# Moving the on-chip buffers of a three-block kernel to multiples of 1024 bytes

## The chip, the core and the metric

The kernel runs on one core of a Trainium2 chip. Its time is the device time in microseconds (us) of one execution, from start to end. TensorE is called PE below, its weight loads PEld, VectorE DVE, ScalarE ACT, GpSimd POOL and SyncE SP. SBUF is the on-chip memory that the compute engines work from, PSUM the memory that matmuls write.

## What is computed

Three transformer-like blocks run one after the other on 256 tokens of width 2048, in fp32, with one layer each: a block with latent attention and a bidirectional recurrence, one with a convolution, pooling, a Fourier mix and a gated MLP, and one with two attentions and a gated MLP. The time goes for the most part into dense products with large weights, such as these two of the second block (the reference, cut):

```python
def first_block(x, g_pre, w_in, ...):
    h = rms_norm(x, g_pre)
    proj = h @ w_in
    ...
def second_block(x, ..., w_gate, w_up, w_down, ...):
    ...
        hid = jax.nn.silu(jnp.einsum("bsd,df->bsf", x, w_gate[i])) * \
            jnp.einsum("bsd,df->bsf", x, w_up[i])
        ffn = jnp.einsum("bsf,fd->bsd", hid, w_down[i])
        ...
def third_block(x, c, positions, w_ada, b_ada, ...):
        mod = jax.nn.silu(c) @ w_ada[l] + b_ada[l]
        ...
        x = x + g2 * conv_ffn(h2, w_up[l], conv_w[l], conv_b[l], w_down[l])
    return rmsnorm(x, final_norm_g)
```

## The kernel before

Activations stand with features on the 128 partitions and the 256 tokens along the row, so a chunk of 128 features is 128 x 256 fp32 values, 1024 bytes in each partition. Nearly all activations live in one large SBUF array, `work`; functions `w(at, ...)` and `own(name, at, ...)` cut named pieces out of it, `at` in fp32 words from its start. `own` gives a piece a tensor of its own at the same address, mostly of type fp32r, the reduced fp32 format in which PE takes one pass over the columns.

Weights come in slots of 8192 bytes per partition (1 MB in all) through a ring of four slots, `ring`. SP issues the transfer of slot n when PE has used slot n - 4. Where the product is split (lines 442 to 444, function `by_parts`), ACT rounds each half slot to fp32r into `ring_hi` (line 1054), DVE subtracts that from the weights and leaves the rest in place of them, in `ring_parts`, which is the ring under a second type (line 1569). The activations are split in the same way into a `_hi` and a `_lo` tensor. Each tile of 128 x 128 weights then takes three fp32r matmuls of 256 columns, in the order L442 (high weights by high activations), L443 (high weights by low activations), L444 (low weights by high activations), each with a load of its own weights before it, four column tiles m for each of 16 or 44 chunks. The other dense products (`by_feature`, line 414, and the gates in line 603) are plain fp32 out of the ring. Weights are the stationary operand and activations the moving one.

The 24 us to 300 us of the run are the first block's input products in split form (moving `h1_hi`, `h1_lo`, weights `ring_hi1` and `ring_parts`); 480 to 1100 us the recurrence in a loop over eight pairs of heads, small fp32 matmuls (lines 629 to 721) between ACT and DVE; 1110 to 1500 us plain fp32 products and the convolution; from 1540 us to the end split products again, with `mix_hi`, `x_hi`, `hid_hi`, `hs_hi` and `h_hi` as moving operands and `ring_hi` as weights. In three stretches POOL fetches 96 tiles `work<-in_ada` of 1 MB, on which DVE works in line 1584.

All orders are written out by hand: each engine's program is a fixed sequence with semaphores, and addresses take no part in it. The allocator `sb(...)` hands out SBUF from the bottom up, each buffer at a multiple of 32 bytes; the order of the calls in the code sets the addresses.

Of the kernel before, what the change touches and what calls it, by code (L numbers as in the profile page):

```python
# [17 lines left out]
P = 128  # L18
T = 256
D = 2048  # L20
DC = D // P
COLS = 512
KPS = 4
SLOT = KPS * COLS
# [23 lines left out]
TRI = 384  # L48
# [70 lines left out]
NPAR = [sum(w for _, w in b) for b in PARAMS]  # L119
# [21 lines left out]
N_CONST = max(N_1, N_3 + 4 * T)  # L141
# [57 lines left out]
def build_program(nc, a):  # L199
# [3 lines left out]
    def sb(name, shape, dt=F32):  # L203
        return ctx.enter_context(nc.sbuf_tensor(name, shape, dt))
# [6 lines left out]
        return sems[name]  # L211


    ring_at = -(-nc.sbuf_base // 32) * 32
    ring = sb("ring", [P, RING, SLOT])
    ring_parts = nc.alloc_sbuf_tensor_at("ring_parts", [P, RING, SLOT], F32R, offset=ring_at)
    CON = sb("con", [P, N_CONST])
    PR = sb("par", [P, max(NPAR)])
    X = sb("resid", [P, DC, T])
    MOD = sb("mod", [P, 96])  # L220
    RED = sb("red", [P, 2, T])
    STD = sb("std", [P, 2, T])
    work_at = -(-nc.sbuf_base // 32) * 32
    W = sb("work", [P, WORK])
    PS = ctx.enter_context(nc.psum_tensor("ps", [P, 8, 512], F32))

    def w(at, *shape):

        n = int(np.prod(shape))
        v = W[:, at:at + n]  # L230
        names = "abcde"[:len(shape)]
        if len(shape) == 1:
            return v
        return v.rearrange(f"p ({' '.join(names)}) -> p {' '.join(names)}", **{k: s for k, s in zip(names[1:], shape[1:])})

    def own(name, at, *shape, dt=F32R):


        return nc.alloc_sbuf_tensor_at(name, [P, *shape], dt, offset=work_at + 4 * at)[:]

    def con(name, n, at=0):
        off = {**OFF_ALL, **OFF_1, **OFF_3}[name]
        return CON[:, off + at:off + at + n]

    def par(name, k=0, n=1):
        return PR[:, PAR[name] + k:PAR[name] + k + n]

# [29 lines left out]
    H1_LO = [own("h1_lo0", 12288, 8, T), own("h1_lo1", 29184, 8, T)]  # L277
    NKK = X[:, 0:8, :]
    TW = X[:, 8:12, :]
    SG1 = X[:, 12:16, :]  # L280
    LW = X[:, 14:16, :].rearrange("p a (b n) -> p (a b) n", b=2)

# [39 lines left out]
    GU, GU2, GU3 = w(30720, 4, T), w(31744, 4, T), own("gu", 32768, 4, T, dt=F32)  # L322
    P2, P2_HI, P2_LO = w(33792, 2, T), own("p_hi", 34304, 2, T), own("p_lo", 33792, 2, T)
    BROW = w(20736, 2 * COLS)
    HI = own("ring_hi", 35504, 4, SLOT // 2)


    Q_SB, K_SB, V_SB = w(4096, 8, T), w(6144, 8, T), w(8192, 2, WIDTH)
# [2 lines left out]
    SBB = w(15424, 4, 4, TRI)  # L331
    ROT = CON[:, N_3:N_3 + 4 * T].rearrange("p (c t) -> p c t", t=T)
    TURN, TURNI, ANG = w(30720, 4, T), w(30720, 4, T).bitcast(I32), w(31744, 4, T)
    TURN_IX, TURN_DS = w(8192, 4, T), w(17472, 4, T)
    REL = w(25664, 4, TRI)
    LG, PTR = [w(25664, 4, TRI), w(21568, 4, TRI)], [w(27200, 4, TRI), w(23104, 4, TRI)]
    SCORE, LEFT, SBIAS = w(29760, TRI), w(30144, TRI), w(30528, TRI)
    TOP, SM3 = w(30912, 8), w(30920, 64)
    O3, O3_LO = w(31008, DC, T), own("o3_lo", 31008, DC, T)
    SQ3 = w(15424, DC, T)  # L340
    NORM3 = w(4096, DC, T)
    HS_HI = own("hs_hi", 21568, DC, T)
    HID3_HI, HID3_LO = own("hid3_hi", 4096, FF3_CHUNKS, T), own("hid3_lo", 15360, FF3_CHUNKS, T)
    H3_HI, H3_LO = own("h3_hi", 26624, DC, T), own("h3_lo", 0, DC, T)
    UP3 = w(30720, 8, T + 2)
# [19 lines left out]
    def _(sp):  # L365
        for k in range(4):
            sp.dma_start(X[:, 4 * k:4 * k + 4, :], a["x"][:, 4 * k:4 * k + 4, :]).then_inc(S(f"x_loaded{k}"), 16)
        for k in range(RING):
# [17 lines left out]
    def _(pe):  # L386
# [90 lines left out]
        def sum_over_features(bank, k):  # L477

            t.wait(S("red_ready"), 1)
            t.give(mm(PS[:, bank, 0:T], ones, RED[:, k, :], start=True, stop=True), S("sum_ready"))  # L480

# [10 lines left out]
        def sum_reduced(bank, k):  # L492


            t.wait(S("red_ready"), 1)
            mm(PS[:, bank, 0:T], ones, RED[:, k, :], start=True, stop=False)

# [258 lines left out]
        sum_chunks(4, SQ, 12, 4, False, True)  # L756
        xc = lambda k: X[:, k, :]

# [267 lines left out]
    def _(act):  # L1026
# [34 lines left out]

        act.dma_start(CON[:, 0:N_ALL], a["const1"][:, 0:N_ALL]).then_inc(S("first_loaded"), 16)
        act.dma_start(PR[:, 0:NPAR[0]], a["params1"]).then_inc(S("first_loaded"), 16)
        for k in range(4):
            act.wait_ge(S(f"x_loaded{k}"), 16)
            t.give(A(SQ[:, 4 * k:4 * k + 4, :], X[:, 4 * k:4 * k + 4, :], ACT.Square), S("squared"))
        act.dma_start(CON[:, N_ALL:N_1], a["const1"][:, N_ALL:N_1]).then_inc(S("const_loaded"), 32)
        act.wait_ge(S("first_loaded"), 32)
# [179 lines left out]
        act.wait_ge(S("x_ready"), DC)  # L1248
        act.dma_start(PR[:, 0:NPAR[1]], a["params2"]).then_inc(S("params_loaded"), 16)
        act.dma_start(CON[:, N_ALL:N_3], a["const3"]).then_inc(S("params_loaded"), 16)  # L1250
        act.dma_start(P2, a["p"]).then_inc(S("params_loaded"), 16)
# [84 lines left out]
        act.wait_ge(S("x1_ready"), 2 * DC)  # L1336
        act.dma_start(PR[:, 0:NPAR[2]], a["params3"]).then_inc(S("params_loaded"), 16)

        def modulated(n, shift, hi):

            for k in range(DC):
                act.wait_ge(S("scaled"), (2 + n) * DC + k + 1)
                A(hi[:, k, :], NORM3[:, k, :], ACT.Identity, bias=MOD[:, shift + k:shift + k + 1])
                A(H[:, k, :], NORM3[:, k, :], ACT.Identity, bias=MOD[:, shift + k:shift + k + 1]).then_inc(S("h3_ready"), 1)
                if n == 0 and k in (7, 11):
# [148 lines left out]
    def _(gp):  # L1494
# [22 lines left out]
        with gp.Fori(0, PAIRS) as i:  # L1517
            gp.wait_ge(S("stage_free"), i + 1)
            gp.nop()
            for dst, src in ((RC, RR_), (KC, KK_), (NC_, NKK)):  # L1520
                gp.tensor_copy(dst, src[:, bass.ds(i, 1), :].rearrange("p a t -> p (a t)"))
            gp.tensor_copy(PP, PR[:, bass.ds(PAR["pair"] + i * 8, 8)])
            gp.tensor_copy(VD, VV_[:, bass.ds(i, 1), :].rearrange("p a (c s) -> p (a c) s", s=CH).unsqueeze(2)
# [14 lines left out]
    def _(v):  # L1538
# [8 lines left out]
        def add_chunks(src, n, k):  # L1547

            t.give(v.tensor_reduce(RED[:, k, :], src.rearrange("p c t -> p t c"), AX.X, ALU.add), S("red_ready"))

# [26 lines left out]
        def modulation(first, count):  # L1577


            for n in range(first, first + count):  # L1580
                run, slot, loads = ADA_AT[n]
                x = ADA[run][0][slot]
                v.wait_ge(S(f"ada_loaded{slot}"), 16 * loads)
                v.tensor_tensor_reduce(x, x, ADA[run][1], 1.0, 0.0, ALU.mult, ALU.add, MOD[:, n:n + 1])\  # L1584
                    .then_inc(S("ada_used"), 1)
# [313 lines left out]
        for j in range(2):  # L1899
# [10 lines left out]
            with v.Fori(0, TAPS - 1) as i:  # L1910
                for m in range(4):
                    c = 4 * j + m
                    v.wait_ge(S("conv_step"), i * 4 + (4 * TAPS * j + m + 1))
                    stt(ACC[:, c, :], W[:, bass.ds(i + (c * (T + TAPS - 1) + 1), T)],
                        PR[:, bass.ds(i * 8 + (PAR["taps"] + 8 + c), 1)],
                        ACC[:, c, :], ALU.mult, ALU.add).then_inc(S("conv_step"), 1)
# [31 lines left out]
        v.wait_ge(S("ada_used"), ADA_COLUMNS)  # L1948
        t.give(tt(MOD[:, :], MOD[:, :], par("b_ada", 0, 96), ALU.add), S("mod_ready"))
        def angles(part):  # L1950
# [105 lines left out]
        for gain, at_ in (("n1_g", 16), ("n2_g", 64)):  # L2056
            ins = stt(MOD[:, at_:at_ + DC], MOD[:, at_:at_ + DC], 1.0, par(gain, 0, DC), ALU.add, ALU.mult)
        step(ins)

        def scaled_norm(n, at_, hi):  # L2060

            invert(0)
            for k in range(DC + 2):
                if k < DC:
                    t.give(stt(NORM3[:, k, :], X[:, k, :], MOD[:, at_ + k:at_ + k + 1], STD[:, 0, :], ALU.mult, ALU.mult),
                           S("scaled"))
# [487 lines left out]
```

## Time and profile before

| | |
|---|---|
| median of 3 runs | 3747.72 us (3746.31 to 3749.8) |
| profiled execution, its own time | 3751.21 us |
| its span, first to last instruction | 3749.9 us |
| mean granted TensorE clock | 0.983 |
| PE busy / PEld busy | 3567.7 / 3365.8 us |
| DVE busy / ACT busy | 2232.4 / 1410.3 us |
| DMA, mean | 174 GB/s |

The profile is of one execution. The matmuls of PE are pipelined and their ends are modelled: 280 ns is how long one is in the array, not how often one starts. How often one starts is read from the starts in the timeline, or from the number of matmuls in a window in which PE never waits.

### The profile page before, as it was taken

To read this page: it belongs to the slowest core of one execution; us is meant where nothing else is said; L and a number is where in the kernel's file an instruction comes from. 1 tells how busy PE (TensorE), PEld (TensorE's weight loads), DVE (VectorE), ACT (ScalarE), POOL (GpSimd) and SP (SyncE) were. 2 spreads that over 40 slices of the span, in tenths; PEclk is the share of its full clock that TensorE was granted. 3 is DMA by queue.
4 is the path that set the end of the run, shared out by engine and by line. 5 is a ranking of instruction groups with operands and counts; after the bars stand their busy time and mean duration, and the time that the engine had idled before them with its cause. 6 is when DMAs were issued, how large, how long until landed. Compare 5 with 4: busy or idle time off the path is not lost.

```text
span 3749.9 us, 63400 instructions
## 1 busy us (share of the span) xinstructions
PE 3567.7 (95%) x26060; PEld 3365.8 (90%) x26060; DVE 2232.4 (60%) x3034; ACT 1410.3 (38%) x1688; POOL 76.1 (2%) x155
## 2 busy tenths in 40 slices
PE   8997889999999999889999999998998999999998
PEld 8996788888888886689999999997987899999998
DVE  7865455555447569765555554455566667777545
ACT  5441123332220000454444433345355454444443
POOL 0000000000000100000000000000000000000000
PEclk9999999999999999989999999999999999999999
DMA  8647611111137984435555555553442455555554
GB/s 309 258 172 301 233 52 67 57 48 48 59 122 275 385 330 164 146 134 180 186 183 190 181 192 193 193 185 113 160 154 96 156 185 183 190 180 189 191 188 151
DMA packets 91728, 654.13 MB, mean 174 GB/s; under 512 B 10177, under 2 KB 10817, under 8 KB 13122
## 3 DMA queue, kind: packets, MB, share of 16 engines
q1 hardware_dynamic: 74736, 540.05, 40.2%
q0 software_dynamic: 14256, 103.82, 7.0%
q10 hardware_dynamic: 2594, 8.15, 0.6%
q8 instruction: 116, 1.90, 0.2%
q14 instruction: 26, 0.21, 0.0%
HBM read 649.88 MB, written 2.10 MB: 174 GB/s over the span
## 4 chain that ended last, share of the span: by engine, by line
PE 88%; DVE 6%; ACT 3%; issue 1%; DMA 1%; ACTq 0%; DVEq 0%
PE ps L442 19%; PE ps L444 19%; PE ps L443 19%; PE ps L414 11%; PE ps L603 6%; PE ps L677 2%; PE ps L665 2%; PE ps L473 1%; PE ps L488 1%; DVE ring_parts L1569 1%; DMA work<-in_ada 1%; PE ps L721 1%; PE ps L712 1%; ACT work L1216 1%; DVE work L1584 0%
## 5 line engine op out<-in xcount | busy, mean ns | idle before, releaser
L1569 DVE TENSOR_TENSOR ring_parts<-ring,ring_hi 128x1024 fp32r<-128x1024 f32 x810 | 977.0, 1223 | 792.4 <-ACT ring_hi L1054 781.8
L1054 ACT ACTIVATE ring_hi<-ring 128x1024 fp32r<-128x1024 f32 x810 | 852.3, 1061 | 1102.8 <-PE ps L444 1090.9
L443 PE MATMUL ps<-h_lo,ring_hi 128*128 128x256 f32 x2624 | 735.4, 280 | 0.0
L442 PE MATMUL ps<-h_hi,ring_hi 128*128 128x256 f32 x2112 | 598.7, 283 | 26.7 <-DVE ring_parts L1569 22.3
L444 PE MATMUL ps<-h_hi,ring_parts 128*128 128x256 f32 x2112 | 595.0, 282 | 0.0
L443 PEld LDWEIGHTS ps<-h_lo,ring_hi 128*128 128x128 f32 x2624 | 496.6, 189 | 1.4 <-issue 1.2
L442 PE MATMUL ps<-x_hi,ring_hi 128*128 128x256 f32 x1664 | 467.2, 281 | 5.8 <-DVE x_lo L1591 4.5
L444 PE MATMUL ps<-x_hi,ring_parts 128*128 128x256 f32 x1664 | 467.3, 281 | 0.0
L443 PE MATMUL ps<-x_lo,ring_hi 128*128 128x256 f32 x1664 | 463.6, 279 | 0.0
L442 PEld LDWEIGHTS ps<-h_hi,ring_hi 128*128 128x128 f32 x2112 | 400.4, 190 | 29.9 <-DVE ring_parts L1569 24.5
L444 PEld LDWEIGHTS ps<-h_hi,ring_parts 128*128 128x128 f32 x2112 | 401.2, 190 | 0.0
L444 PE MATMUL ps<-hid_hi,ring_parts 128*128 128x256 f32 x1392 | 390.1, 280 | 0.0
L442 PE MATMUL ps<-hid_hi,ring_hi 128*128 128x256 f32 x1392 | 389.8, 280 | 0.0
L443 PE MATMUL ps<-hid_lo,ring_hi 128*128 128x256 f32 x1392 | 387.0, 278 | 0.0
L442 PEld LDWEIGHTS ps<-x_hi,ring_hi 128*128 128x128 f32 x1664 | 312.9, 188 | 6.4 <-issue 4.8
L414 PE MATMUL ps<-work,ring 128*128 128x256 f32 x1440 | 313.7, 380 | 2.6 <-DVE work L1873 2.6
L443 PEld LDWEIGHTS ps<-x_lo,ring_hi 128*128 128x128 f32 x1664 | 313.1, 188 | 0.0
L444 PEld LDWEIGHTS ps<-x_hi,ring_parts 128*128 128x128 f32 x1664 | 312.2, 188 | 0.0
L414 PEld LDWEIGHTS ps<-work,ring 128*128 128x128 f32 x1440 | 274.4, 191 | 42.1 <-DVE work L1873 3.0
L1584 DVE CUSTOM_DVE_ANT_0 work<-work 128x2048 f32<-128x2048 f32 x96 | 218.6, 2289 | 85.3 <-DMA work<-in_ada 85.2
L443 PEld LDWEIGHTS ps<-hid_lo,ring_hi 128*128 128x128 f32 x1392 | 261.0, 188 | 0.0
L442 PEld LDWEIGHTS ps<-hid_hi,ring_hi 128*128 128x128 f32 x1392 | 260.8, 187 | 0.0
(422 smaller groups left out, 5420.2 us busy)
## 6 DMA issues: line engine op xcount, KB each, us to landing
ring<-in_weights SPq DMA_DIRECT2D x511, 1024.0 KB, 4.8
work<-in_ada POOLq DMA_DIRECT2D x96, 1024.0 KB, 9.0
work<-in_c_row POOLq DMA_DIRECT2D x3, 1024.0 KB, 4.9
resid<-in_lora ACTq DMA_DIRECT2D x9, 256.0 KB, 2.6
resid<-in_x SPq DMA_DIRECT2D x4, 512.0 KB, 6.8
resid<-in_x ACTq DMA_DIRECT2D x1, 2048.0 KB, 13.9
out<-work SPq DMA_DIRECT2D x4, 512.0 KB, 2.9
con<-in_const ACTq DMA_DIRECT2D x1, 1536.0 KB
```

Of the source, the lines that this page charges most:

```text
L414: ins = mm(PS[:, b + m // 2, (m % 2) * T:(m % 2 + 1) * T], ws[:, k, m * P:(m + 1) * P], rhs(kc), start=(kc == 0 and m % 2 == 0), stop=(kc ...
L442: mm(o, w_hi[:, k, cols], hi(kc), start=(kc == 0 and m % 2 == 0), stop=False, skip_group_check=True)
L443: mm(o, w_hi[:, k, cols], lo(kc), start=False, stop=False, skip_group_check=True)
L444: ins = mm(o, w_lo[:, 2 * half + k, cols], hi(kc), start=False, stop=(kc == last - 1), skip_group_check=True)
L473: ins = mm(PS[:, b + m, :], lhs(kc, m), ws[:, k, :], start=(kc == 0 and not biased), stop=(kc == per * KPS - 1), skip_group_check=True)
L488: ins = mm(PS[:, bank, 0:T], ones, src[:, k, :], start=(begin and k == first), stop=(end and k == first + count - 1))
L603: ins = mm(PS[:, m // 2, (m % 2) * T:(m % 2 + 1) * T], ws[:, k, m * P:(m + 1) * P], H[:, kc, :], start=(kc == 0 and m % 2 == 0), stop=(kc ...
L665: ins = mm(PS[:, 2 + 3 * d, c * P:(c + 1) * P], LS[:, d, c, :], XY[:, d, 0, c, :], start=True, stop=True)
L677: ins = mm(PS[:, 3 + 3 * d, c * P:(c + 1) * P], XY[:, d, 1, c, :], ZS[:, d, c, :], start=True, stop=True)
L1054: A(high_ring(n)[:, 2 * (e % 2) + half, :], ring[:, n % RING, half * (SLOT // 2):(half + 1) * (SLOT // 2)], ACT.Copy)\
L1569: tt(lo, x, high_ring(n)[:, e % 4, :].bitcast(F32), ALU.subtract).then_inc(S("lo_ready"), 1)
L1584: v.tensor_tensor_reduce(x, x, ADA[run][1], 1.0, 0.0, ALU.mult, ALU.add, MOD[:, n:n + 1])\
```

## The change

The calls that allocate SBUF stand in another order. The small buffers (`mod`, `par`, `con`) come first, then a pad of 544 bytes that nothing uses, then `red`, `std`, `resid`, the ring and the work area, and these five begin at multiples of 1024 bytes. Inside the work area four regions that did not begin at a multiple of 256 words from its start are moved to one: `HI` (the tensor `ring_hi`), the score buffers at 25664 and 21568, `O3`/`O3_LO`, and `HS_HI` with the second pair of score buffers. Each engine's instructions, their order, shapes and waits are the same in both programs; only addresses differ.

```diff
-    ring_at = -(-nc.sbuf_base // 32) * 32
+    MOD = sb("mod", [P, 96])
+    PR = sb("par", [P, max(NPAR)])
+    CON = sb("con", [P, N_CONST])
+    pad = -(-(-nc.sbuf_base // 32) * 32) % 1024 // 4
+    if pad:
+        sb("pad", [P, pad])
+    RED = sb("red", [P, 2, T])
+    STD = sb("std", [P, 2, T])
+    X = sb("resid", [P, DC, T])
+    ring_at = nc.sbuf_base
     ring = sb("ring", [P, RING, SLOT])
     ring_parts = nc.alloc_sbuf_tensor_at("ring_parts", [P, RING, SLOT], F32R, offset=ring_at)
-    CON = sb("con", [P, N_CONST])
-    PR = sb("par", [P, max(NPAR)])
-    X = sb("resid", [P, DC, T])
-    MOD = sb("mod", [P, 96])
-    RED = sb("red", [P, 2, T])
-    STD = sb("std", [P, 2, T])
-    work_at = -(-nc.sbuf_base // 32) * 32
+    work_at = nc.sbuf_base
     W = sb("work", [P, WORK])
+    assert ring_at % 1024 == 0 and work_at % 1024 == 0
...
-    HI = own("ring_hi", 35504, 4, SLOT // 2)
+    HI = own("ring_hi", 35328, 4, SLOT // 2)
...
-    REL = w(25664, 4, TRI)
-    LG, PTR = [w(25664, 4, TRI), w(21568, 4, TRI)], [w(27200, 4, TRI), w(23104, 4, TRI)]
+    REL = w(25856, 4, TRI)
+    LG, PTR = [w(25856, 4, TRI), w(21760, 4, TRI)], [w(27392, 4, TRI), w(23296, 4, TRI)]
...
-    O3, O3_LO = w(31008, DC, T), own("o3_lo", 31008, DC, T)
+    O3, O3_LO = w(31232, DC, T), own("o3_lo", 31232, DC, T)
...
-    HS_HI = own("hs_hi", 21568, DC, T)
+    HS_HI = own("hs_hi", 21760, DC, T)
```

Where the tensors stand, by the two built programs (bytes in a partition, and the remainder to 1024):

| tensor | before | remainder | after | remainder |
|---|---|---|---|---|
| ring, ring_parts | 1152 | 128 | 37888 | 0 |
| con | 33920 | 128 | 3488 | 416 |
| par | 47296 | 192 | 1536 | 512 |
| resid | 49248 | 96 | 21504 | 0 |
| red | 66016 | 480 | 17408 | 0 |
| work | 70112 | 480 | 70656 | 0 |
| ring_hi1 (first block) | 143840 | 480 | 144384 | 0 |
| h1_hi, h1_lo | 160224, 119264 | 480 | 160768, 119808 | 0 |
| x_hi, x_lo, mix_*, hid_*, h3_* | 160224 ... | 480 | 160768 ... | 0 |
| ring_hi (blocks two and three) | 212128 | 160 | 211968 | 0 |
| hs_hi | 156384 | 736 | 157696 | 0 |
| o3_lo | 194144 | 608 | 195584 | 0 |

A tile of 128 weight columns is 512 bytes, so column tiles with odd m stand 512 bytes further: `ring_hi` then has remainders 160 and 672 before, 0 and 512 after. In the recurrence the tiles XY, LS and ZS stand behind a buffer of 8 words, so they begin at multiples of 64 bytes before and 32 bytes past one after; the other tiles of `work` do the reverse.

## Rows read from the trace of the kernel before

**Rows 1.** The page's head: span, busy time of each engine, granted clock in 40 slices.

```profile
span 3749.9 us, 63400 instructions
PE 3567.7 (95%) x26060; PEld 3365.8 (90%) x26060; DVE 2232.4 (60%) x3034; ACT 1410.3 (38%) x1688; POOL 76.1 (2%) x155
PEclk9999999999999999989999999999999999999999
```

**Rows 2.** The page's chain of work that ended last, shares of the span.

```profile
PE 88%; DVE 6%; ACT 3%; issue 1%; DMA 1%; ACTq 0%; DVEq 0%
```

**Rows 3.** One line's instructions: L443, matmuls, by operand; min/median/max ns, first and last start.

```profile
L443 PE MATMUL ps<-h_lo,ring_hi x2624: 277/279/420, 24.5 to 3491.3; 128*128 128x256 f32 x188
...
L443 PE MATMUL ps<-x_lo,ring_hi x1664: 277/279/416, 1670.0 to 2456.3; 128*128 128x256 f32 x185
...
L443 PE MATMUL ps<-hid_lo,ring_hi x1392: 277/278/279, 2196.6 to 3734.4; 128*128 128x256 f32 x199
...
L443 PE MATMUL ps<-mix_lo,ring_hi x256: 277/279/416, 1552.1 to 1643.5; 128*128 128x256 f32 x128
...
L443 PE MATMUL ps<-o_lo,ring_hi x256: 276/281/283, 2886.7 to 2976.8; 128*128 128x256 f32 x128
...
L443 PE MATMUL ps<-p_lo,ring_hi x32: 277/278/279, 2193.8 to 2459.1; 128*128 128x256 f32 x32
```

**Rows 4.** Windows (start:end, length, busy and count by engine, clock, DMA share, GB/s).

```profile
core 0: us, PE busy (x) PEld busy (x) DVE busy (x) ACT busy (x) POOL busy (x), PEclk, DMA share, GB/s
60.00:100.00 40.00, 40.00 (x342) 40.00 (x341) 29.56 (x26) 15.97 (x17) 2.65 (x5) 1.00 0.89 334
2000.00:2400.00 400.00, 400.00 (x3398) 400.00 (x3398) 202.98 (x169) 167.76 (x158) 0.00 (x0) 1.00 0.54 190
2905.00:2975.00 70.00, 70.00 (x597) 70.00 (x596) 40.33 (x38) 28.53 (x28) 0.00 (x0) 1.00 0.54 190
```

**Rows 5.** The window 1250:1300, plain fp32 matmuls of L414, same columns.

```profile
1250.00:1300.00 50.00, 50.00 (x233) 44.03 (x232) 29.85 (x26) 3.88 (x4) 6.35 (x12) 1.00 1.01 421
```

**Rows 6.** Timeline of PE at 2900 us (start, us in the array, line, operands).

```profile
2899.91 0.29 PE L444 MATMUL ps<-hs_hi,ring_parts 128*128 128x256 f32 x1
2900.03 0.28 PE L442 MATMUL ps<-hs_hi,ring_hi 128*128 128x256 f32 x1
2900.16 0.28 PE L443 MATMUL ps<-o_lo,ring_hi 128*128 128x256 f32 x1
2900.27 0.28 PE L444 MATMUL ps<-hs_hi,ring_parts 128*128 128x256 f32 x1
2900.39 0.28 PE L442 MATMUL ps<-hs_hi,ring_hi 128*128 128x256 f32 x1
```

**Rows 7.** One line each: durations min/median/max of DVE and ACT work.

```profile
L1914 DVE SCALAR_TENSOR_TENSOR work<-work,par x240: 466/474/481, 1417.8 to 1515.6; 128x256 f32<-128x256 f32 x120
L1569 DVE TENSOR_TENSOR ring_parts<-ring,ring_hi x810: 1160/1225/1230, 22.8 to 3726.0; 128x1024 fp32r<-128x1024 f32 x162
L1054 ACT ACTIVATE ring_hi<-ring x810: 1039/1061/1072, 18.9 to 3724.9; 128x1024 fp32r<-128x1024 f32 x162
```

**Rows 8.** Groups by line and shape: busy us, mean ns, idle before.

```profile
L2270 DVE TENSOR_TENSOR uc<-uc 128x1024 f32<-128x1024 f32 x11 | 13.5, 1225 | 0.4
L1476 ACT ACTIVATE work<-uc 128x1024 f32<-128x1024 f32 x11 | 11.7, 1065 | 0.1
```

**Rows 9.** Matmuls of the recurrence, by line: min/median/max ns.

```profile
L665 PE MATMUL ps<-work x640: 275/275/348, 507.0 to 1077.2; 128*128 128x128 f32 x160
L670 PE MATMUL ps<-con,work x256: 272/273/273, 513.8 to 1078.1; 128*128 128x128 f32 x128
L629 PE MATMUL ps<-work x128: 272/275/275, 497.4 to 1050.7; 128*128 128x128 f32 x128
```

**Rows 10.** DMA in the window 320:400: GB/s in 40 slices of 2 us.

```profile
GB/s 57 418 49 0 66 274 258 406 422 365 385 406 414 426 426 426 426 422 422 426 422 418 410 418 266 299 414 365 385 176 422 8 0 33 299 193 0 127 410 418
```

**Rows 11.** Who waited for whom: us in total, times, longest us.

```profile
DVE work L1584 <- DMA work<-in_ada: 85.2, 52, 5.4
...
PEld ps L442 <- DVE ring_parts L1569: 29.3, 15, 7.4
```

## The prediction, made before the changed kernel was run

> **What bounds the kernel now.** The page's head first: PE is busy for 3567.7 of 3749.9 us at almost full clock, DVE for 60% and ACT for 38% [rows 1]. The chain of work that ended last agrees: 88% of it is PE, 6% DVE, 3% ACT, 1% DMA [rows 2]. So what counts is how often a matmul starts. The change leaves every instruction, its place and its waits as they are. It can move the time only through what an address does: to PE's two reads of SBUF (moving operand and next weights), to the reads and writes of DVE and ACT, or to where DMA lands.
>
> The rows then tell how many matmuls are exposed and how long one step takes. L443 stands for one of the three matmuls of each split tile; its six groups count 2624 + 1664 + 1392 + 256 + 256 + 32 = 6224 [rows 3], so there are 3 x 6224 = 18672 split matmuls of 256 columns. A step is the time from one start to the next, and the windows without a wait give it. In 2000 to 2400 us there are 3398 [rows 4]; each is in the array for about 0.28 us, so 0.28 / 0.118 = 2.4 of them began before the window. 400 / 3395.6 = 117.8 ns. The split matmuls thus take 18672 x 0.1178 = 2200 us, 59% of the span. The plain fp32 matmul of the same shape, which takes two passes over its columns, steps at 50 / (233 - 1.8) = 216.3 ns [rows 5], 108.1 ns a pass. A split matmul is one pass and takes 9.7 ns more than that. This surplus is the only thing in the profile that an address could be behind and that is large: 18672 x 9.7 ns = 181 us.
>
> **The change part by part.** *PE, split matmuls.* The trace already holds a natural experiment, since the operands stand differently in the three windows of [rows 4]. In 60:100 the moving tensors and `ring_hi1` have the same remainder to 1024 (480), so the offset between the two reads is 0 or 512 for two of three products. In 2000:2400 it is 480 against 160 or 672. In 2905:2975 the moving operands are at 736 and 608, the weights at 160 and 672. In all three, `ring_parts` is at 128 or 640. Their steps: 40 / (342 - 2.4) = 117.8, 117.8, and 70 / (597 - 2.4) = 117.7 ns. Three relations of moving to stationary address, one step. Inside a pattern of three the gaps do differ, 0.11, 0.12 and 0.13 us in [rows 6], but they make up for each other. Weights at a multiple of 64 bytes (`ring_parts`) and 32 bytes past one (`ring_hi`) both occur in each window, and the mean of the three lines is what is fixed. What the trace doesn't show is a moving operand of a 256-column split matmul at a multiple of 64, 256 or 1024: all stand 32 bytes past a multiple of 64. I bound this unseen case by the nearest rows: below by the pass of the plain matmul (108.1 ns, so -181 us), above by the gaps in [rows 6], 0.12 as the typical high one (+2.2 ns x 18672 = +41 us) and 0.13 as the extreme (+12.2 ns, +228 us). I take 0, since three of three relations gave the same step.
>
> *PE, plain matmuls.* In [rows 5] the moving operand is 32 bytes past a multiple of 64, the weights are 128 past a multiple of 1024, and a pass is already 108.1 ns, the shortest step here; nothing is left to gain. 0.
>
> *PE in the recurrence.* Here some tiles lose their place: XY, LS and ZS leave multiples of 64 while the rest of `work` reaches them. L665 reads only the former, L629 only the latter, both 275 ns for the same shape [rows 9]: 0 either way. The constants leave a multiple of 64 too. Transposes that move `con` show 273 ns against 275 [rows 9]; if they lose those 2 ns, with 256 of L670 and some 190 others of its kind (estimate), the loss is 450 x 2 ns = 0.9 us. I take +0.5.
>
> *DVE and ACT.* L1914, the convolution, reads its input at an offset that steps by 4 bytes through 30 places; all 240 take between 466 and 481 ns [rows 7]. So an offset of DVE is worth at most 15 ns in 474 and no multiple of 64 stands out. For the largest group: L1569, 1225 ns with the ring at a multiple of 64 and `ring_hi` off it [rows 7], against L2270, same shape, everything off it, 1225 ns [rows 8]. ACT: L1054 reads the ring, 1061 ns [rows 7]; L1476 reads `uc` off it, 1065 ns [rows 8]. 4 ns x 810 splits is 3 us of ACT time at most, and PE waits for the split only 29.3 us in all [rows 11]. What hides it is that PE's steps set the pace; if that cover went, the whole of it would be 3 us. 0 for both.
>
> *DMA.* All destinations move from 96 to 224 past a multiple of 256 to one; only the constants, loaded a few times, do not. Rates with the old places reach 421 GB/s in [rows 5] and 426 in [rows 10]. DMA sets the end in 1% of the chain, 37 us [rows 2], mostly where DVE waits for `in_ada`, 85.2 us in all [rows 11] with PE waiting behind DVE for part of it. The two peak rates differ by 1.2%; a like change would be worth 0.4 us of 37. I take -0.4, ends -1.2 and 0.
>
> By the Trainium skill (DMA: Bandwidth & Descriptors, "How a descriptor splits into AXI transactions") a transaction must start at a multiple of 256 bytes, and a descriptor that doesn't start there costs one more, with bytes fetched for nothing. For the 8 KB row of a slot that would be 33 pieces instead of 32, and 3% of the DMA share would be an estimated 1.1 us; no row here can tell, as no large transfer lands at such a multiple. For operands of the engines the Trainium skill (SBUF — State Buffer, "Operand start alignment") asks only for multiples of the element size and says that "these runs timed nothing", so it doesn't settle PE's case.
>
> *Sum.* 0 + 0 + 0.5 + 0 - 0.4 = 0 us. Against the profiled execution, 3751.2 us (span 3749.9 and 1.3 around it), this is 3751; that execution lies 3.5 us, 0.1%, above the median of the runs, so the forecast for the median is 3747.7, rounded to 3747.5.
>
> **The rivals.** *A, faster: the surplus of 9.7 ns comes of the moving operand's start, 32 bytes past a multiple of 64.* For it: every split matmul in the trace has that start and every one has the surplus, and one-pass columns ask twice as much of the read as two-pass ones, which don't show it. Against it: plain matmuls start at the same place without loss, and the stationary operand's place doesn't matter. Time: if all of it went, 3747.7 - 181 = 3567; if half, 3657. DVE and ACT would keep up: per half slot PE has 24 steps, 2.8 us, and DVE needs 1.2.
>
> *B, slower: PE's two reads now meet.* After the change moving operand and weights of all three products start at the same place modulo 512 bytes. If SBUF gave way to one read at a time there, each load would hold up the columns. For it: the gaps in [rows 6] show that a step does depend on the places. Against it: 60:100, where two of three pairs already stand so, at 117.8. Price: steps of 0.12 us, +41 us, 3789. It decides from 0.4 ns a step on, since 18672 x 0.4 ns = 7.5 us is 0.2%.
>
> *C, slower by little: the small losses add up.* Constants off their multiple (+0.9), ACT's 4 ns where nothing hides them (+3), and a conflict on the DVE side that no row shows; +4 to +12 us, 3752 to 3760.
>
> *D, the change does nothing,* because the addresses aren't what the code says. The built program has them as in the table; this would give the forecast's time anyway.
>
> **How the numbers follow.** About 0.2% is what a measurement of this kernel can tell from no change, here 7.5 us. Forecast, with D: 0.75. A: 0.13, since the only unseen place is the one that the change makes, and a surplus is there to be explained. B: 0.06. C: 0.06, half of it beyond 0.2%. Faster 0.14 (A and a DMA gain larger than I think), slower 0.10, same 0.76. The predicted time is the forecast's, 3747.5. Forecast and C together hold 0.81, so the range is theirs: down to 3735 for gains of DMA and of a small part of A's surplus (0.6 ns a step), up to 3762 for C's end. A in full and B are the up to 2 in 10 left out.
>
> **What would show it.** The windows 2000:2400 and 60:100 again: 3398 and 342 matmuls if I am right; A would show more than 3410 in the first, up to 3700, B fewer than 3385. The gaps inside the pattern of three may well change while their mean stays. L1569 at 1225 and L1054 at 1061 ns; L670 at 273 or 275. Between 320 and 400 us the DMA rate would peak at 426 GB/s. By the Trainium skill's rule on 256 bytes (DMA: Bandwidth & Descriptors, the same section) it would peak at an estimated 426 x 33/32 = 439. I am wrong if a one-pass read has a penalty for its start that two-pass reads hide.

## The result and the profile after

The changed kernel takes 3791.48 us (3789.26 to 3794.61, four runs) against 3748.76 us for the kernel before (3746.31 to 3752.5): a ratio of 1.0114, 95% interval 1.0096 to 1.0131. It is 43 us slower where no change was forecast. The head of its page answers to [rows 1]:

```profile
span 3793.3 us, 63400 instructions
...
PE 3611.8 (95%) x26060; PEld 3409.6 (90%) x26060; DVE 2233.9 (59%) x3034; ACT 1408.3 (37%) x1688; POOL 76.0 (2%) x155
...
PE 88%; DVE 6%; ACT 3%; issue 1%; DMA 1%; ACTq 0%; DVEq 0%
```

The same instructions; PE is busy 44.1 us longer and the span is 43.4 us longer, DVE and ACT are as before, and the chain has the same shape as in [rows 2]. So the time is in PE's steps. The windows say where; 2000:2400 and 60:100 answer to [rows 4], 1250:1300 to [rows 5], in the same columns:

```profile
60.00:100.00 40.00, 40.00 (x336) 40.00 (x335) 29.40 (x26) 15.97 (x17) 2.65 (x5) 1.00 0.88 332
2000.00:2400.00 400.00, 400.00 (x3335) 400.00 (x3334) 202.49 (x169) 166.62 (x157) 0.00 (x0) 1.00 0.52 186
1250.00:1300.00 50.00, 50.00 (x234) 44.02 (x233) 29.70 (x26) 3.88 (x4) 6.61 (x13) 1.00 1.01 418
```

In 400 us without a wait there are 3335 split matmuls where there were 3398: a step is 400 / (3335 - 2.4) = 120.0 ns instead of 117.8. The first block has 336 for 342, 119.9 ns. The plain matmuls are where they were (234 for 233). 18672 x 2.2 ns = 41 us, and 3748.8 + 41 = 3790 for a measured 3791.5: this one step is nearly the whole result, and it is the price of rival B.

What the forecast said of the other parts held within a few us. DVE's and ACT's splits, the transposes that move the constants, and what DVE waits for (the line of L1569 is now L1573, and so on, four further):

```profile
L1573 DVE TENSOR_TENSOR ring_parts<-ring,ring_hi 128x1024 fp32r<-128x1024 f32 x810 | 978.4, 1224 | 829.0 <-ACT ring_hi L1058 818.0
L1058 ACT ACTIVATE ring_hi<-ring 128x1024 fp32r<-128x1024 f32 x810 | 850.5, 1057 | 1142.3 <-PE ps L448 1129.8
...
L674 PE MATMUL ps<-con,work x256: 272/273/273, 521.0 to 1085.3; 128*128 128x128 f32 x128
...
DVE work L1588 <- DMA work<-in_ada: 84.3, 51, 4.9
```

The 1224 and 1057 ns in the first two lines are means. The medians, to be set beside [rows 7], are 1225 ns for DVE in both kernels and 1058 for ACT where they were 1061. The convolution's instructions on DVE have a median of 479 ns for the 474 of [rows 7].

### The profile page after: what moved, and what is told of

Same layout as the page of the kernel before. It is cut to its first block, busy times and chain, and to the rows that moved or that the text cites. A ratio compares the mean times of both kernels' runs of the same rounds, so it can differ in the third digit from the quotient of the medians.

```text
span 3793.3 us, 63400 instructions
## 1 busy us (share of the span) xinstructions
PE 3611.8 (95%) x26060; PEld 3409.6 (90%) x26060; DVE 2233.9 (59%) x3034; ACT 1408.3 (37%) x1688; POOL 76.0 (2%) x155
## 4 chain that ended last, share of the span: by engine, by line
PE 88%; DVE 6%; ACT 3%; issue 1%; DMA 1%; ACTq 0%; DVEq 0%
PE ps L446 19%; PE ps L448 19%; PE ps L447 19%; PE ps L418 11%; PE ps L607 6%; PE ps L681 2%; PE ps L669 2%; PE ps L477 1%; PE ps L492 1%; DVE ring_parts L1573 1%; DMA work<-in_ada 1%; PE ps L725 1%; PE ps L716 1%; ACT work L1220 1%; DVE std L1557 0%
## 5 line engine op out<-in xcount | busy, mean ns | idle before, releaser
L1573 DVE TENSOR_TENSOR ring_parts<-ring,ring_hi 128x1024 fp32r<-128x1024 f32 x810 | 978.4, 1224 | 829.0 <-ACT ring_hi L1058 818.0
L1058 ACT ACTIVATE ring_hi<-ring 128x1024 fp32r<-128x1024 f32 x810 | 850.5, 1057 | 1142.3 <-PE ps L448 1129.8
L447 PE MATMUL ps<-h_lo,ring_hi 128*128 128x256 f32 x2624 | 746.4, 284 | 0.0
L447 PEld LDWEIGHTS ps<-h_lo,ring_hi 128*128 128x128 f32 x2624 | 507.6, 193 | 1.3 <-issue 1.2
L447 PE MATMUL ps<-x_lo,ring_hi 128*128 128x256 f32 x1664 | 472.0, 284 | 0.0
L446 PEld LDWEIGHTS ps<-h_hi,ring_hi 128*128 128x128 f32 x2112 | 409.5, 194 | 29.6 <-DVE ring_parts L1573 23.9
L448 PEld LDWEIGHTS ps<-h_hi,ring_parts 128*128 128x128 f32 x2112 | 409.3, 194 | 0.0
L446 PEld LDWEIGHTS ps<-x_hi,ring_hi 128*128 128x128 f32 x1664 | 320.5, 193 | 6.4 <-issue 4.8
L448 PEld LDWEIGHTS ps<-x_hi,ring_parts 128*128 128x128 f32 x1664 | 320.5, 193 | 0.0
L1588 DVE CUSTOM_DVE_ANT_0 work<-work 128x2048 f32<-128x2048 f32 x96 | 218.7, 2289 | 84.6 <-DMA work<-in_ada 84.3
```

The lines of the kernel that those rows point to most:

```text
L446: mm(o, w_hi[:, k, cols], hi(kc), start=(kc == 0 and m % 2 == 0), stop=False, skip_group_check=True)
L447: mm(o, w_hi[:, k, cols], lo(kc), start=False, stop=False, skip_group_check=True)
L448: ins = mm(o, w_lo[:, 2 * half + k, cols], hi(kc), start=False, stop=(kc == last - 1), skip_group_check=True)
L1058: A(high_ring(n)[:, 2 * (e % 2) + half, :], ring[:, n % RING, half * (SLOT // 2):(half + 1) * (SLOT // 2)], ACT.Copy)\
L1573: tt(lo, x, high_ring(n)[:, e % 4, :].bitcast(F32), ALU.subtract).then_inc(S("lo_ready"), 1)
```

## The experiments

Two kinds of kernel were run. The first moves single buffers of the changed kernel. The second holds nothing but rows of fp32r matmuls at chosen places; there a "pace" is the mean distance from one start to the next in the later part of a row, from the 13th matmul on. It is worked out from the starts in the trace, which are kept to 1 ns where the timeline prints them to 10. In what follows "place" is the remainder of an address to 256 bytes. Each kernel of bare rows was executed once. A whole kernel whose time stands without a range was executed once too; the kernel before took 3746.5 to 3758.6 us beside these runs, so such a time tells 40 us apart but not 5, and the number of matmuls in a window is the better evidence.

**Bare rows over places.** Core of the kernel, one row of 48 matmuls of 256 columns for each pair of places, a plain matmul between rows:

```python
mm(o, wts(so)[:, c * P:(c + 1) * P], mov(mo)[:, 512 * (k % 2):512 * (k % 2) + n], start=True, stop=True,
   skip_group_check=True)
```

> Only the fp32r matmuls are measured here: 48 of them in a row for each pair of places (moving operand and weights each 0, 16, 32, 48, 64, 96, 128 or 160 bytes past a multiple of 4096), with a plain fp32 matmul as a mark between; nothing of the reference is computed, the output is a copy of x. Before: mean step 117.8 ns, after the change: 120.0 ns. Theory M (the moving operand's place modulo 64 decides): 120.0 ns at 0, 64 and 128 whatever the weights, less at 32, 96 and 160. Theory W (the weights' place modulo 64 decides): the same with the roles exchanged. Theory R (the two reads meet, so the difference of the places decides): 120 on the diagonal and less off it. The pattern with the old places (480 with 160, 160, 128) gives 117.8 under all three and 120 if none holds and something around the matmuls matters.

The timeline of PE, a row in one line (start, us from the first start to the end of the last, operands with their places):

```profile
47.73 6.31 PE L73 MATMUL ps<-mov_0b,wts_0b 128*128 128x256 f32 x48
...
60.95 6.24 PE L73 MATMUL ps<-mov_0b,wts_32b 128*128 128x256 f32 x48
...
257.06 6.01 PE L73 MATMUL ps<-mov_64b,wts_0b 128*128 128x256 f32 x48
...
466.34 11.50 PE L73 MATMUL ps<-mov_0b,wts_0b 128*128 128x512 f32 x48
...
478.13 11.75 PE L73 MATMUL ps<-mov_0b,wts_32b 128*128 128x512 f32 x48
```

With nothing else at work on the core, the pace ran from 113.3 ns (moving 64, weights 0) to 120.1. All six pairs of equal places at multiples of 32 gave 120.0 after a few steps, moving and weights both at 32 or both at 96 among them (but so did some unequal pairs, moving 0 with weights 96 for one, and the equal pairs at 16 and 48 gave 118.3), so it isn't the moving operand's own place: theory M falls, and theory W with it (moving 0 with weights 0 gave 120.0, with weights 64 it gave 117.8, though both are multiples of 64). The pair matters. The difference alone does not set the pace either: moving 64 with weights 0 gave 113.3, moving 96 with weights 32 gave 117.8. Rows of 512 columns show it with the opposite sign, 227 ns at equal places and 233 at places 32 apart; rows of 128 columns do not show it, 111.7 to 111.8 ns in all four. The three sets of old places gave 117.8, 117.7 and 117.9, near the 117.8 of the kernel.

**The work area 32 bytes further.**

```diff
+    sb("shift", [P, 8])
     work_at = nc.sbuf_base
```

> The changed kernel with the work area alone 32 bytes further: activations and ring_hi 32 bytes past a multiple of 64 again, ring_parts and the ring stay at a multiple of 1024. The difference of moving and weight places stays 0 or 512 for two of three products and becomes 32 for the third. Theory M and theory W: back to 117.8 ns a step, about 3750 us. Theory R: 119 to 120 ns, 3775 to 3792 us.

3751.69 us, ratio to the kernel before 1.0003 (0.9994 to 1.0013), step 117.8 ns in every stage. Read alone this would have settled on theory M or W. Two of the three products still have equal places here, so theory R in the form in which I wrote it down, a loss for each product whose own two places are equal, predicted too much: with one product of the three at unequal places none of the 2.2 ns is lost.

**The ring 32 bytes lower.**

```diff
-    if pad:
-        sb("pad", [P, pad])
+    sb("pad", [P, pad - 8])
...
+    sb("shift", [P, 8])
     work_at = nc.sbuf_base
```

> The changed kernel with ring, resid, red and std 32 bytes lower: ring_parts 32 bytes past a multiple of 64, all activations and ring_hi at one. Theory M: still 120.0 ns, 3791 us. Theory W: the loads of one product in three change place, 118.5 to 119.3 ns, 3764 to 3779 us. Theory R: one product in three no longer meets, the same 118.5 to 119.3 ns.

3748.35 us, 117.8 ns. Here every activation in the work area and `ring_hi` still stand at a multiple of 1024, as in the changed kernel; of the operands of the split matmuls `ring_parts` alone moved against them. So the moving operand's place by itself is not the cause, and theory M is out. Theories W and R had 118.5 to 119.3 ns, and neither was met: two of three products still have equal places, as in the run before, and nothing is lost.

**The work area 32 further, and `ring_hi` another 32.**

```diff
+    sb("shift", [P, 8])
...
-    HI = own("ring_hi", 35328, 4, SLOT // 2)
+    HI = own("ring_hi", 35336, 4, SLOT // 2)
```

> As the work area 32 bytes further, and ring_hi of the second and third block another 32: moving operands 32 bytes past a multiple of 64, all weights of those blocks at one, differences 32 or 544. Theory M: 117.8 ns or less in 2000 to 2400 us, 3750 us or less. Theory W: 120.0 ns, 3785 us. Theory R: about 117.8, since no pair meets.

3753.97 us; 118.25 ns a step in the second and third block and 117.8 in the first. No theory had named a value between 117.8 and 120.0 here. The window 2000:2400 of the work area 32 bytes further, of the ring 32 bytes lower, and of this run:

```profile
2000.00:2400.00 400.00, 400.00 (x3399) 400.00 (x3398) 202.35 (x169) 168.10 (x159) 0.00 (x0) 1.00 0.53 189
```

```profile
2000.00:2400.00 400.00, 400.00 (x3399) 400.00 (x3398) 201.87 (x168) 168.69 (x159) 0.00 (x0) 1.00 0.54 191
```

```profile
2000.00:2400.00 400.00, 400.00 (x3386) 400.00 (x3385) 201.78 (x169) 167.58 (x158) 0.00 (x0) 1.00 0.53 189
```

**Bare rows in the kernel's own order.**

```python
product("mov_hi", h, "wts_hi", hi, k % 4)
product("mov_lo", l, "wts_hi", hi, k % 4)
product("mov_hi", h, "wts_lo", lo, k % 4)
```

> Only rows of fp32r matmuls of 256 columns, output a copy of x; nothing of the reference is computed. First 32 rows of 48 with the moving operand at 0 and the weights at 0, 32, ... 992 bytes past a multiple of 1024, then 32 rows with the roles exchanged, then three pairs of places each six times with other work between, then the kernel's own order (high weights by high activations, high weights by low, low weights by high) for six sets of places and for a grid of 64 places of the two weights, with the low activations at 0 and at 64. Theory R (the difference of the two places decides): each row depends on moving minus weights place alone, 120.0 ns at 0, 117.8 at -64, 118.3 at -32, and is periodic; the sets of the changed kernel, of the work area 32 bytes on, and of that with ring_hi another 32 on give 120.0, 117.8 and 118.25, and the old places 117.8. Rival H (what came before decides which of two paces a row falls into): the pairs 64 with 0 and 96 with 32, which had 113.3 and 117.8 ns in the run before although their difference is the same, change their pace with the work between.

First the 32 single rows with the moving operand at 0 and the weights at 0, 32, 64, ... In the timeline the rows from 256 on repeat those from 0 on. Shown are those with the weights at 32, 64, 96, then 224, 256, 288 and 320:

```profile
46.58 6.23 PE L56 MATMUL ps<-mov_hi,wts_hi 128*128 128x256 f32 x48
53.10 6.03 PE L56 MATMUL ps<-mov_hi,wts_hi 128*128 128x256 f32 x48
59.43 6.26 PE L56 MATMUL ps<-mov_hi,wts_hi 128*128 128x256 f32 x48
...
85.66 6.17 PE L56 MATMUL ps<-mov_hi,wts_hi 128*128 128x256 f32 x48
92.12 6.31 PE L56 MATMUL ps<-mov_hi,wts_hi 128*128 128x256 f32 x48
98.72 6.23 PE L56 MATMUL ps<-mov_hi,wts_hi 128*128 128x256 f32 x48
105.25 6.03 PE L56 MATMUL ps<-mov_hi,wts_hi 128*128 128x256 f32 x48
```

The paces, worked out from the starts, with a period of 256 bytes through all four repeats:

| weights minus moving place | 0 | 32 | 64 | 96 | 128 | 160 | 192 | 224 |
|---|---|---|---|---|---|---|---|---|
| ns, moving at 0 | 120.0 | 118.3 | 113.3 | 118.7 | 118.7 | 119.9 | 117.8 | 116.8 |
| ns, weights at 0 | 120.0 | 118.4 | 113.3 | 117.3 | 118.7 | 119.9 | 117.8 | 116.7 |

So within these rows the period of 256 held, but not quite "the difference alone" (at 96 the two rows of the table differ by 1.4 ns). Rival H's own test came out against it: moving 64 with weights 0, 96 with 32 and 320 with 256 kept 117.8 ns in all 18 rows, whatever ran between. Yet moving 64 with weights 0 had run at 113.3 in the rows over places, and moving 0 with weights 64, here 113.3, at 117.8 there. The first line is from those rows, the second from these, at the same two places:

```profile
257.06 6.01 PE L73 MATMUL ps<-mov_64b,wts_0b 128*128 128x256 f32 x48
...
456.93 6.22 PE L56 MATMUL ps<-mov_hi,wts_hi 128*128 128x256 f32 x48
```

The two kernels differ in where the tensors stand beyond the last 256 bytes, and the first lets the moving operand alternate between two addresses 2048 bytes apart. No run tells which of this matters; places modulo 256 are not the whole story.

Then the sets. In this order of products the bare rows give what the whole kernel gives: 120.0 for the changed kernel's places, 117.8, 117.8 and 118.2 for the runs above (kernel: 117.8, 117.8 and 118.25), and 117.8 for both sets of old places. So these paces need neither ACT nor DVE nor DMA. Windows of 10 us in the first two sets, the changed kernel's places and those of the work area 32 bytes further:

```profile
579.00:589.00 10.00, 10.00 (x86) 10.00 (x85) 0.00 (x0) 0.00 (x0) 1.00 0.00 0
591.00:601.00 10.00, 10.00 (x87) 10.00 (x86) 0.00 (x0) 0.00 (x0) 1.00 0.01 2
```

The grid over the two weights' places, with all activations at 0, reaches from 113.3 to 121.1 ns; 31 of its 64 cells lie between 117.7 and 117.9, ten at 119.9 or more, five below 117. With the low activations at 64 it reaches from 116.6 to 122.3. A few cells of the first grid:

| ring_hi | ring_parts | ns a step |
|---|---|---|
| 0 | 0 (changed kernel) | 120.0 |
| 192 | 160 (before, blocks two and three) | 117.8 |
| 64 | 192 | 113.3 |
| 192 | 64 | 113.3 |
| 32 | 128 | 121.1 |

**Two sets of places that the grid calls fast.**

```diff
-    if pad:
-        sb("pad", [P, pad])
+    sb("pad", [P, pad - 16])
...
+    sb("shift", [P, 16])
     work_at = nc.sbuf_base
...
-    HI = own("ring_hi", 35328, 4, SLOT // 2)
+    HI = own("ring_hi", 35344, 4, SLOT // 2)
```

> The changed kernel with the ring (ring_parts) 64 bytes lower, at 192 past a multiple of 256, and ring_hi of blocks two and three 64 bytes higher; all activations and ring_hi1 stay at multiples of 1024. Theory R (places modulo 256 alone set the step, as in the rows of bare matmuls, where these places gave 113.3 ns): 113.3 ns in 1700 to 2500 us and in the third block, 117.8 in the first; 16560 steps of 4.4 ns less than before, 73 us, so about 3677 us. Rival H (the steady pace of bare rows is lost when ACT, DVE, DMA and waits come in, and another takes over): 117.8 ns and 3750 us.

3687.51 us (3677.53 to 3688.08, five runs), ratio 0.9824 (0.9809 to 0.9839): faster than the kernel before by 1.8%, and than the changed kernel by 2.7%. Steps of 113.3 ns through nearly all of blocks two and three (a short stretch after 2500 us has some at 118), 117.8 in the first block as forecast. Windows of it in the first, second and third block:

```profile
60.00:100.00 40.00, 40.00 (x342) 40.00 (x341) 30.02 (x26) 15.98 (x17) 2.65 (x5) 1.00 0.90 336
2000.00:2400.00 400.00, 400.00 (x3531) 400.00 (x3531) 208.96 (x175) 173.98 (x164) 0.00 (x0) 1.00 0.55 197
...
3200.00:3400.00 200.00, 200.00 (x1762) 199.82 (x1761) 148.60 (x205) 104.20 (x98) 0.00 (x0) 1.00 0.54 192
```

3531 matmuls for 3335 in the same 400 us. The gain is 62 us where 73 were expected. Four of the five runs, the profiled one among them, had a mean granted clock of 0.979 or 0.980; the fifth had 0.985 and took 3677.5 us, as expected. The kernel before, run beside it, took 3747.0 and 3748.0 us in its two runs at 0.985 and 3758.6 in one at 0.981: at an equal clock the gain is 70 us. So the clock accounts for the rest in size; why it was granted less here was not tried.

```profile
core 0: 3686.2 us, clock 0.980
```

The other set has the ring 192 bytes lower and `HI` at 35376:

> As before with the ring 192 bytes lower (at 64 past a multiple of 256) and ring_hi 192 bytes higher. Theory R: 113.3 ns again in blocks two and three, 117.8 in the first, about 3677 us. Rival H: 117.8 ns, 3750 us.

3716.37 us, half of the gain. The same places ran at two paces, 113.3 ns from about 1690 to 2480 us and again in most of 2870 to 3060, and 118.9 in most of the rest of blocks two and three. Windows of either kind:

```profile
2200.00:2300.00 100.00, 100.00 (x885) 100.00 (x884) 49.34 (x42) 41.09 (x39) 0.00 (x0) 1.00 0.56 199
...
3200.00:3400.00 200.00, 200.00 (x1684) 200.00 (x1683) 143.24 (x195) 98.84 (x93) 0.00 (x0) 1.00 0.51 184
3500.00:3700.00 200.00, 200.00 (x1685) 200.00 (x1684) 94.34 (x82) 80.46 (x84) 0.00 (x0) 1.00 0.49 174
```

Neither forecast of this run came true. Rival H was right that a row's steady pace can give way to another in the kernel (to 118.9 ns, not to the 117.8 it named); for the first set theory R was right.

**One part undone: `ring_hi` back at its old place in the work area.**

```diff
-    HI = own("ring_hi", 35328, 4, SLOT // 2)
+    HI = own("ring_hi", 35504, 4, SLOT // 2)
```

> The changed kernel with one part undone: ring_hi of blocks two and three again at its old place in the work area, 704 bytes further, 192 past a multiple of 256. Theory R: 120.0 ns in the first block as in the changed kernel, 117.8 in blocks two and three (bare row with weights at 192 and 0), about 3755 us. If the ring's or the small buffers' place were the cause: 120.0 everywhere, 3791 us.

3751.39 us. The first block keeps the changed kernel's 336 matmuls in 60:100 (119.9 ns), the others are back at 3399 in 2000:2400:

```profile
60.00:100.00 40.00, 40.00 (x336) 40.00 (x335) 29.25 (x26) 15.97 (x17) 2.65 (x5) 1.00 0.89 334
2000.00:2400.00 400.00, 400.00 (x3399) 400.00 (x3398) 201.95 (x169) 168.22 (x159) 0.00 (x0) 1.00 0.53 189
```

One line of the diff out of several gives back nearly all of the 43 us: with it `ring_hi` of blocks two and three does not stand at the activations' place. The first block's 2112 steps of 2.2 ns, about 5 us, stay lost.

**The ring 256 bytes lower.** As the ring 32 bytes lower, with 64 words for 8.

> The changed kernel with the ring, resid, red and std 256 bytes lower. Theory R with its period of 256 bytes: nothing changes, 120.0 ns and 3791 us. If multiples of 1024 matter, or the distance of ring and work area itself: another step, towards 117.8 ns.

3790.77 us, 120.0 ns in all stages. Of the split matmuls' operands only `ring_parts` moved against the others, by 256 bytes, and nothing changes, as a period of 256 has it; the loss does not need the ring at a multiple of 1024:

```profile
2000.00:2400.00 400.00, 400.00 (x3336) 400.00 (x3335) 202.43 (x169) 166.31 (x158) 0.00 (x0) 1.00 0.53 187
```

**From many starts.**

> Bare fp32r matmuls in the kernel's own order, output a copy of x, nothing of the reference computed. Four sets of places of the two weights (64 and 192, 192 and 64, 0 and 0, 192 and 160 past a multiple of 256, activations at one), each 16 times, with a plain fp32 matmul of 32, 64, ... 512 columns ahead, so that each row starts from another point. Theory R alone (places set the pace): each set has one pace, 113.3, 113.3, 120.0 and 117.8 ns. Theory R with H (places allow one or two paces, the start chooses): the second set, which had 113.3 and 118.9 ns in the kernel, shows both here; the first and the third show one.

| ring_hi, ring_parts | paces of the 16 rows, ns |
|---|---|
| 64, 192 | 113.3 in all |
| 192, 64 | 118.9 and 113.3 in turn, eight each |
| 0, 0 | 120.0 in all |
| 192, 160 | 117.8 in all |

Two neighbouring rows of the second set differ only in that the plain matmul ahead has 32 or 64 columns. Windows of 5 us in each of them:

```profile
196.00:201.00 5.00, 5.00 (x44) 5.00 (x44) 0.00 (x0) 0.00 (x0) 1.00 0.00 0
205.50:210.50 5.00, 5.00 (x47) 5.00 (x46) 0.00 (x0) 0.00 (x0) 1.00 0.00 0
```

The places thus allow one steady pace or two, and where there are two, what ran before chooses. Whether it is the length of the matmul ahead is not shown: the columns rise by 32 from row to row, so "every other length" and "every other row" are the same here. One pace for the first fast set and two for the second fit what the two did in the kernel; no run follows the switch there.

**A set that the grid calls slow, though no two places are equal.** The ring 128 bytes lower and `HI` at 35336.

> The changed kernel with the ring 128 bytes lower and ring_hi of blocks two and three 32 bytes higher. Theory R, read from the grid of bare rows: 121.1 ns in blocks two and three and 118.9 in the first, (16560 x 3.3 + 2112 x 1.1) ns more than the kernel before, 57 us, about 3806 us, slower than the changed kernel although its places differ from one another. A theory by which only equal places cost: 117.8 ns, 3750 us.

3784.76 us (3781.06 to 3801.15), ratio 1.0104 (1.0076 to 1.0133). Slow without equal places, so "the reads meet" is no rule by which to tell good from bad. The size was missed by 21 us: block two has the 121.1 ns of the grid, but its last product falls in part, and the third block almost wholly, into a pace of 118.2 that the one bare row of this set had not shown. The first block ran at 119.1 for a forecast of 118.9.

```profile
2000.00:2400.00 400.00, 400.00 (x3305) 400.00 (x3304) 200.24 (x168) 165.58 (x156) 0.00 (x0) 1.00 0.51 185
3200.00:3400.00 200.00, 200.00 (x1694) 200.00 (x1693) 144.26 (x196) 98.73 (x93) 0.00 (x0) 1.00 0.51 184
```

## Why the prediction was wrong

**What bounds the kernel:** right. PE's steps decide, and the 18672 split matmuls times the change of their step are 41 of the 43 us.

**PE, split matmuls: this is the step that failed,** in the sentence "I take 0, since three of three relations gave the same step". The three windows were taken as a sample of all relations. Measured from the moving high operand, modulo 256, they are `ring_hi` 0 with `ring_parts` 160, and twice 192 with 160 (the third with its low activations 128 further). The first and the second are cells of the grid, 117.8 each, and 117.8 is what about half of its cells have. The trace of before held three draws from the commonest value. The case that the change makes, all three differences 0, was in none of them, and it steps at 120.0. I named the right bound (+2.2 ns, +41 us) and gave it no weight.

Against rival B I held that in 60:100 two of three products already stand at equal places without loss. The observation was right and the conclusion wrong: costs don't add up product by product. The work area 32 bytes further and the ring 32 bytes lower each leave two equal pairs, and both give 117.8, while three equal pairs give 120.0. The pattern of three as a whole sets the pace. Rival B named the arrangement and its price (3789 for a measured 3791.5), and it had a chance of 0.06. Its own picture, one read giving way to the other, is not shown, and as a rule it fails: there are slow sets without equal places.

**The gaps in [rows 6]** of 0.11 to 0.13 us were read as the bounds of the unseen case. The rows are rounded to 10 ns, and rounding alone can make such gaps: the changed kernel, whose starts kept to 1 ns lie 119 to 121 ns apart in 2000:2400, shows 0.11 to 0.13 too:

```profile
2199.84 0.28 PE L448 MATMUL ps<-x_hi,ring_parts 128*128 128x256 f32 x1
2199.97 0.28 PE L446 MATMUL ps<-x_hi,ring_hi 128*128 128x256 f32 x1
2200.09 0.28 PE L447 MATMUL ps<-x_lo,ring_hi 128*128 128x256 f32 x1
2200.20 0.28 PE L448 MATMUL ps<-x_hi,ring_parts 128*128 128x256 f32 x1
2200.32 0.28 PE L446 MATMUL ps<-x_hi,ring_hi 128*128 128x256 f32 x1
```

That +2.2 ns came out right is therefore partly luck, and the extreme of 0.13 us was in no gap. But the gaps of the kernel before do differ beneath the rounding. Its starts at 2900 us are 113, 119, 121, 122, 114, 118, 116, 120 and 117 ns apart, and then the same nine again, three tiles of three products; in 2000:2400 they range from 113 to 121. The changed kernel has lost the short ones. So the reading that steps depend on the places was right, and the sentence that the gaps "make up for each other" should have been a warning that a step is no sum of independent costs.

**Rival A** was wrong in its reason (the moving operand's start) and right in that the surplus over 108.1 ns depends on addresses: 4.4 of the 9.7 ns went in the first fast set. No row of 256 columns went below 113.3. The yardstick itself, a plain matmul as two passes, no row of before showed; the bare rows bear it out, where a plain matmul of 512 columns steps at 429 ns and a one-pass one at 227 to 233.

**PE, plain matmuls and the recurrence:** right, 216 ns and 275 ns stayed. The 0.5 us put down for the constants was not there: the transposes take 273 ns as in [rows 9], off their multiple of 64 bytes.

**DVE and ACT:** right; medians of 1225 ns in both and 1058 for 1061. The convolution on DVE is 5 ns slower at the median, 479 for 474, but its place is not the reason: in the first fast set, where the work area stands as in the changed kernel, it has 475, and ACT's rounding has 1062.

**DMA:** hardly anything to be seen of a gain. In 1250:1300, where DMA is full, 418 GB/s after and 421 before [rows 5]; a packet of 8 KB takes 309 ns at the median in both, and DVE waits for `in_ada` 84.3 us for 85.2 [rows 11]. The peak between 320 and 400 us, which the forecast had as its sign, is of no use: one slice of 2 us reached 438 GB/s where 426 had been the highest, but the slices scatter more after the change, and in 345:367, where DMA is full, the mean went from 422 to 425. By the Trainium skill's rule on starts at multiples of 256 bytes (DMA: Bandwidth & Descriptors, "How a descriptor splits into AXI transactions") I estimated 3%. The trace doesn't agree for these writes of 8 KB rows into SBUF; their source addresses weren't changed or looked at.

**The chances.** Slower had 0.10 and the range ended at 3762. The unseen case had been bounded at +41 us by the prediction's own working and then left out of the range, although it was not unlikely: it is exactly the arrangement that the diff makes.

**What stays open.** Why the addresses change the pace is not shown, nor that one read waits for the other; the runs show that the pace depends on both operands' places, on the three products taken together and on what ran before, and two kernels of bare rows disagree by 4.5 ns on one pair of places. Why the best pace is 113.3 and not 108.1 is open too; at 512 columns the least of six rows is 226.7, twice as much, so what is left over 108.1 for each 256 columns (5.2 ns) doubled with the columns and was no fixed cost of each load. The first block, which needs other buffers moved, was left at its pace.

## What to carry to other kernels

Where one-pass matmuls of 256 columns with a fresh load each set the pace, the places of moving operand and weights are a parameter to be measured, worth 113 to 121 ns a step, and "everything at a round address" was among the slow sets. Measure the kernel's own order of products in bare rows, from several starts, and prefer a set of places that shows a single pace. Then look at the windows of the kernel itself: one set that ran at 121.1 ns in its bare row fell to 118.2 in a whole block. When a trace seems to say that a parameter doesn't matter, count which of its values the trace holds before giving the unseen one the same result.

## What the runs showed of the hardware

- Steps of fp32r matmuls of 128 x 128 weights by 256 columns, no other engine at work: 113.3 to 122.3 ns by where the operands stand, 120.0 in every row with all operands at equal places modulo 256 that are multiples of 32 (118.3 at 16 and at 48). Shifts of one operand by 256 bytes changed nothing within 1024. At 512 columns 227 ns at equal places and 233 at 32 apart; at 128 columns 111.7 to 111.8 in all four tried.
- The same places can hold two paces (113.3 and 118.9 ns), and rows of the same instructions in one kernel fell into either in turn.
- Between the two layouts plain fp32 matmuls of 256 columns kept 216 ns and DVE's split of 128 x 1024 its 1225 ns; ACT's went from 1061 to 1058, and was 1062 in the first fast set.
- `ring_hi` 64 bytes higher and the ring 64 bytes lower take the changed kernel from 3791 to 3688 us.
